# Weights' stream laid out in order of use and loaded two units at a time

## What is computed

```
proj = rms_norm(x, norm1_g) @ w_in
x = x + (sigmoid(ga) * (y_diff @ w_diff_o) + sigmoid(gb) * (y_fox @ w_fox_o)) @ w_out
q = rms_norm(x, norm2_g) @ w_query           # 8 heads, two halves of 128
s = einsum(q, sub_keys); top 16 of 128 in each half, top 16 of the 256 sums
act = gelu(t . expert_u[e]);  x = x + sum_e gate_e * act_e * expert_v[e]     # 8 * 16 = 128 experts a token
...
```

```
x_l = half_ffn(x_l); x_c = half_ffn(x_c)      # 1024 -> 2816 -> 1024, silu gate, adaptive shift and scale
h = rmsnorm(x) * (1 + scale) + shift
y = fourier_na_mixer(h_l, h_c)  in layer 0, mla_mixer(h_l, h_c) in layer 1
x = x + gate * y;  half_ffn again
...
return rmsnorm(x_l, final_g)
```

## Time and profile before

| | |
|---|---|
| median of 3 runs | 3260.35 us (3255.09 to 3262.51) |
| the profiled execution's own time | 3251.68 us |
| its span in the trace | 3249.5 us |
| PE, PEld, DVE, ACT, POOL busy | 91%, 74%, 73%, 31%, 40% |
| moved by DMA | 1003.54 MB, mean 309 GB/s |
| layer 0, gather stage | about 248 to 1066 us |
| layer 1, gather stage | about 1309 to 2176 us |
| second block, latent stream | about 2176 us to the end |

### The profile page before, as it was taken

One profiled execution on the slowest core, in us unless ns is written; L12 is line 12 of the kernel. 1 busy time (PEld: TensorE's weight loads), 2 busy tenths in 40 slices (PEclk: granted clock), 3 DMA queues, 4 the chain that ended last, 5 costly groups with the idle time before them and its releaser, 6 DMA issues. The chain is left out here.

```text
span 3249.5 us, 43549 instructions
## 1 busy us (share of the span) xinstructions
PE 2965.4 (91%) x15748; PEld 2389.1 (74%) x15748; DVE 2362.0 (73%) x4772; ACT 1013.7 (31%) x2036; POOL 1311.5 (40%) x1213
## 2 busy tenths in 40 slices
PE   8998989887887899989997998959999999999998
PEld 5876656564544587767765776729997999997898
DVE  5776777777886776777778877777754787856574
ACT  2422311111241242221111111135455544445543
POOL 1106776677777211667776777660000010000000
PEclk9999999999998999999998999969999999999999
DMA  9659999999999867999999999987761787851453
GB/s 355 224 199 383 360 409 409 409 409 406 385 391 389 327 235 272 373 385 409 409 409 408 395 409 409 408 330 233 232 227 45 243 284 231 274 170 66 158 185 99
DMA packets 276500, 1003.54 MB, mean 309 GB/s; under 512 B 31952, under 2 KB 32752, under 8 KB 276032
## 3 DMA queue, kind: packets, MB, share of 16 engines
q0 software_dynamic: 173696, 635.85, 50.7%
q1 hardware_dynamic: 100944, 361.15, 31.2%
q10 hardware_dynamic: 1648, 3.78, 0.3%
HBM read 999.57 MB, written 1.05 MB: 308 GB/s over the span
## 5 line engine op out<-in xcount | busy, mean ns | idle before, releaser
L289 PE MATMUL bank<-hT,ring 128*128 128x256 f32 x3744 | 835.4, 381 | 13.4 <-ACT hT L929 9.5
L289 PEld LDWEIGHTS bank<-hT,ring 128*128 128x128 f32 x3744 | 714.2, 191 | 142.8 <-issue 37.9
L415 POOL DMA_INDIRECT gring<-in_expert_u,idx x512 | 658.3, 1286 | 376.0 <-PE bank L585 145.0
L1387 DVE CUSTOM_DVE_ANT_0 gring<-gring,t_tok 128x1024 f32<-128x1024 f32 x512 | 611.8, 1225 | 91.0 <-DMA gring<-in_expert_u,idx 69.0
L585 PE MATMUL bank<-gring,dg 128*128 128x512 f32 x1012 | 517.4, 657 | 135.9 <-DMA gring<-in_expert_v,idx 108.7
L415 POOL DMA_INDIRECT gring<-in_expert_v,idx x512 | 554.8, 1084 | 175.2 <-issue 151.4
L1706 DVE TENSOR_TENSOR wl<-ring,wr 128x1024 fp32r<-128x1024 f32 x309 | 377.4, 1223 | 209.5 <-ACT wr L1701 209.2
L585 PEld LDWEIGHTS bank<-gring,dg 128*128 128x128 f32 x1012 | 205.1, 210 | 383.8 <-issue 354.9
L1367 DVE SCALAR_TENSOR_TENSOR x<-gring,wts,x 128x1024 f32<-128x1024 f32 x259 | 332.5, 1284 | 210.7 <-DMA gring<-in_expert_v,idx 142.4
L1710 PE MATMUL bank<-hr,wr 128*128 128x258 f32 (+1 forms) x1512 | 430.1, 284 | 0.8 <-DVE hT L1691 0.6
L1712 PE MATMUL bank<-hr,wl 128*128 128x258 f32 (+1 forms) x1512 | 426.7, 282 | 0.0
(11 more groups left out here) (330 smaller groups left out, 3673.1 us busy)
## 6 DMA issues: line engine op xcount, KB each, us to landing
ring<-in_stream SPq DMA_DIRECT2D x679, 512.0 KB
lat_ada<-in_ada POOLq DMA_DIRECT2D x66, 512.0 KB, 5.4
t_tok<-in_ada POOLq DMA_DIRECT2D x56, 512.0 KB, 5.4
gring<-in_ada POOLq DMA_DIRECT2D x56, 512.0 KB, 6.1
gring<-in_expert_u,idx POOLq DMA_INDIRECT x512
gring<-in_expert_v,idx POOLq DMA_INDIRECT x512
na_bias_sb<-in_na_bias POOLq DMA_DIRECT2D x1, 4096.0 KB, 15.5
x<-in_x SPq DMA_DIRECT2D x2, 512.0 KB, 4.3
```

The lines of the kernel that those rows point to most:

```text
L289: last = pe.matmul(out, w[:, k * P:(k + 1) * P], act_T[:, k, :], start=(k == 0), stop=(k == KD - 1))
L415: pool.indirect_dma_start(out=gring[:, N % GR, :], out_offset=None, in_=table, in_offset=bass.IndirectOffsetOnAxis(ap=idx[:, b, 4 * (Q % 3 ...
L1387: dve.tensor_tensor_reduce(out=rows, in0=rows, in1=t_tok[:, b, :], scale=1.0, scalar=0.0, op0=ALU.mult, op1=ALU.add, accum_out=pre[:, Q % ...
```

## The change

The host now writes `stream` in the order of use: one row for every use, so a unit that is used twice stands there twice, and the rows are put together in pairs, as `[pair, partition, 2, 1024]`. One transfer loads a pair, 8 KB per partition, contiguous in HBM and in SBUF. The ring has eight places, which are four pairs, and one semaphore per pair (`units_full`). SP loads the first four pairs, then the constants, and for every further pair v it waits until both units of pair v-4 are used up. 679 units make 340 transfers, the last with one unit twice. No other engine's instructions change but for the semaphore that is waited for.

```diff
-RING = 9
+RING = 8
+RP = RING // 2
...
-        slot_full = [sem(f"slot_full{i}") for i in range(RING)]
+        units_full = [sem(f"units_full{i}") for i in range(RP)]
...
             u = first[name] + t
-            eng.wait_ge(slot_full[u % RING], 16 * (u // RING + 1))
+            eng.wait_ge(units_full[u // 2 % RP], 16 * (u // RING + 1))
             return ring[:, u % RING, :]
...
-            for u, (row, split, value) in enumerate(order):
-                if u == RING:
+            for v in range((len(order) + 1) // 2):
+                if v == RP:
...
-                if u >= RING:
-                    _, old_split, old_value = order[u - RING]
-                    sp.wait_ge(w_low if old_split else unit_done, old_value)
-                sp.dma_start(ring[:, u % RING, :], io["stream"][row]).then_inc(slot_full[u % RING], 16)
+                if v >= RP:
+                    (split0, value0), (split1, value1) = order[2 * (v - RP):2 * (v - RP) + 2]
+                    if split0 != split1:
+                        sp.wait_ge(w_low if split0 else unit_done, value0)
+                    sp.wait_ge(w_low if split1 else unit_done, value1)
+                at = 2 * (v % RP)
+                sp.dma_start(ring[:, at:at + 2, :], io["stream"][v]).then_inc(units_full[v % RP], 16)
...
-            act.wait_ge(slot_full[u % RING], 16 * (u // RING + 1))
+            act.wait_ge(units_full[u // 2 % RP], 16 * (u // RING + 1))
...
-    io = {"stream": np.concatenate(list(parts.values()), 0)}
+    rows = [place[src] + t for _, src, n, _ in PLAN for t in range(n)]
+    rows += rows[-1:] * (len(rows) % 2)
+    stream = np.concatenate(list(parts.values()), 0)[np.array(rows)]
+    io = {"stream": stream.reshape(-1, 2, P, UW).transpose(0, 2, 1, 3)}
```

More of the change, by code:

```diff
@@ L141, in scored_at, with program @@
     return 2 * b + h if h < EARLY_HEADS else 2 * h + b
-def program(nc, io, place):
+def program(nc, io):
     with ExitStack() as ctx:
@@ L159, in program @@
                 n_raw, n_split = n_raw + (not split), n_split + split
-                order.append((place[src] + t, split, n_split if split else n_raw))
+                order.append((split, n_split if split else n_raw))
         x_in = [sem(f"x_in{b}") for b in range(NB)]
@@ L1613, in program @@
         S0 = tuple(split_before[f"up{F}"] for F in range(4))
-        split_units = [u for u, (_, split, _) in enumerate(order) if split]
+        split_units = [u for u, (split, _) in enumerate(order) if split]
         def late_loads(pool):
@@ L2461, in _layout @@
     io["final_g"] = _cols(v["final_g_2"])
-    return {k_: np.ascontiguousarray(a_) for k_, a_ in io.items()}, place
+    return {k_: np.ascontiguousarray(a_) for k_, a_ in io.items()}
 def kernel(**inputs):
@@ L2467 @@
     from concourse.bass_utils import run_bass_kernel_spmd
-    arrays, place = _layout({k: np.asarray(v) for k, v in inputs.items()})
+    arrays = _layout({k: np.asarray(v) for k, v in inputs.items()})
     nc = bacc.Bacc("TRN2", target_bir_lowering=False, num_devices=1)
@@ L2472 @@
     io["out"] = nc.dram_tensor("out_0", (P, KD, S), F32, kind="ExternalOutput").ap()
-    program(nc, io, place)
+    program(nc, io)
     r = run_bass_kernel_spmd(nc, [{"in_" + n: a for n, a in arrays.items()}], core_ids=[0])
```

## The result

The changed kernel takes **3277.2 us** (median of 5 runs, 3273.9 to 3280.0); the kernel before, run beside it, 3259.0 us (5 runs, 3255.1 to 3262.5). The ratio is 1.0053, 95% interval 1.0039 to 1.0067: 18 us, or 0.53%, slower. The forecast was 3266.5 with a range to 3280; the direction and the range hold, but the loss is three times the forecast one, and the number is nearly that of rival (3). So the question is whether the starved gathers of that rival are the cause, or something else. One execution of a later kernel (single8) took 3971.0 us at a mean granted clock of 0.71 where all others had about 0.96; the ratios leave it out.

What follows compares the result with a forecast made beforehand. DMA was taken to bound the gather stages, PE 8 to 11% behind. Profiled 3251.7 + 13.8 (waits, clock) - 7.5 (larger packets) = 3258.0 us; with 8.7 from profiled to median, 3266.5 was forecast, range 3252 to 3280.

Steps and rivals of the forecast that it cites:

- rival (3): Gather stages: bursts of pairs starve the gathers, raising PE's waits for rows; a tenth gives +12 us, 3278 us; chance 15%.
- The wait at `wq`: Ahead of `wq` 0 and 1, PE stands still for the pair's load: 4.9 us in each layer, 9.8 us together.
- The clock: Behind the new wait at `wq`, PE runs at 0.50 for a while: +2.0 us a layer, +4 us, ends 0 and 5.
- Passes on whole to the first gather: From `wq` through scores and choice to POOL's first gather, no slack: all +13.8 us delays the gather stages, ends 9 and 16.
- Rival (2): PE's later idle times, 8.00 and 5.02 us, absorb the delay, up to 5 to 7 us a layer; chance 25%.
- The DMA's time per byte: Gather stages: 8 KB packets cut the stream's DMA time by 4%, 10.6 us, of which -7.5 us is won; ends 0, -13.
- That they grow: Gather stages: growth of PE's waits for gathered rows was named as a sign that the forecast is wrong.
- Rival (4): Stream transfers: they are cut into 4 KB packets after all, so no gain, 3274 us; chance 5%.
- rival (5): Gather stages: PE takes the DMA's gain back, 3274 us; chance 8%.
- Rival (6): All stream loads: fixed parts paid in line, so halving the loads saves 0.9 us a unit, -180 us, 3080; chance 2%.
- `vv` to `dq` costs nothing: Layer 1 projections: 10.1 us between `vv` 0 and 1 used up and `dq` 0 wanted covers the 7.4 us load.
- The start: First eight units: same order as before, first of a pair seen one unit later, 1.3 us once at most, counted as nothing.

Runs made afterwards that it cites:

- single8: Kernel before with stream stored in order of use and a ring of eight units, each loaded alone: 3255.4 us, +3.9 over the kernel before, ratio 1.0010.
- the repeat: The changed kernel run and profiled once more, no edit, on another chip: 3266.5 us, +15.3 us over the kernel before.
- pair_4k: Changed kernel with a pair's two units one behind the other in HBM, so 1 MB transfers have 4 KB packets: 3268.1 us, +16.7 over the kernel before.
- start_single: Changed kernel with only layer 0's `vv`, the stream's first eight units, loaded one by one: 3266.1 us, +14.9 over the kernel before.
- wq_single: Changed kernel with only the units of `wq` loaded one by one: 3258.0 us, +6.8 over the kernel before, ratio 1.0021.
- layout9: Kernel before with only its stream stored in order of use, nine units loaded alone in 4 KB packets: 3251.0 us, ratio 0.9999.
- triple9: hybrid9 with three units per transfer (12 KB per partition) in the gather stages instead of pairs: 3248.4 us, -2.8 against the kernel before, ratio 0.9990.
- hybrid9: Ring of nine, order-of-use layout, pairs only for units streamed in the gather stages, singles elsewhere: 3245.1 us, 5.7 under the kernel before, ratio 0.9984.
- ou_dq_single: Changed kernel with `ou` 0 and 1 used up first on both blocks, and layer 1's `dq` to `gt` loaded singly: 3251.4 us, +0.6 over the kernel before.
- pairs_dq: single8 with only layer 1's `dq` to `gt` loaded in pairs: 3262.9 us, +12.1 over the kernel before, ratio 1.0036.

## Why the prediction was right or wrong

**The wait at `wq`: right, twice.** 4.9 us were worked out from the hump of one load and the full rate for the second half; 4.89 and 4.92 were measured, 4.87 and 4.85 in the repeat. In the repeat the pair is asked for at 235.20 and PE starts at 240.04. Once PE waits for a load, only the load's own time counts, and that could be read from slices.

**The clock: right in kind and about right in size.** +2.0 us a layer was the forecast, 1.59 (5.32 - 3.73) in the repeat, 1.56 and 2.06 in the first profile. Over all eight such waits (those of pair_4k and start_single too) it is 1.50 to 3.01, mean 1.9. The granted clock was 0.54 in the window of 3.5 us behind the wait, so most of it at 1.2 GHz (0.50 in each us from 240 to 243, 0.90 in the next). After the 0.87 and 0.53 us waits of single8 it stayed at 1.00.

**"Passes on whole to the first gather": right.** wq_single gives back 4.2 us at PE, 4.3 at the gather and 8.5 in the median. Rival (2), that a later idle time takes the delay up, falls, and with it its ground: the 8.00 and 5.02 us of the earlier trace rows were stops of that execution, and the wait that stands near them in the other profiles is one for gathered rows, which come later when the first gather does (the products on them begin at 271.75 in layout9 and at 279.22 in the repeat).

**The DMA's time per byte: right.** From 450 to 750 the stream's queue (packets, MB, share) in layout9, in the changed kernel's repeat, and in triple9:

```profile
q1 hardware_dynamic: 6894, 25.10, 21.0%
```

```profile
q1 hardware_dynamic: 3312, 24.12, 19.4%
```

```profile
q1 hardware_dynamic: 2304, 25.17, 20.0%
```

That is 0.837, 0.804 and 0.795% for each MB: 3.9% less with 8 KB packets, for the 4% that I took, and 5.0% with 12 KB. pair_4k has 20.2% for 24.12 MB, 0.837: it is the packet's size, not the transfer's. By the stage lengths of the table, which scatter, the mean over the seven profiles with 8 KB packets in both stages is 812.6 and 861.0 us, and over the four with 4 KB (layout9, single8, pair_4k, pairs_dq) 814.4 and 864.9: 5.6 us in sum, with some 4 us either way, for the 7.5 forecast. Before and the first profile of the changed kernel are left out for their stops. hybrid9, which has this gain and nothing else, says 5.7 us by medians. So the time per byte was right, and what was kept of it a little less than forecast. The first profile does not show the gain: its two stages are 14 us longer than the repeat's; how much of this its stops make is not shown.

**Starved gathers, rival (3): not the cause,** though its number came close. Its place was the gather stages, and these are shorter with 8 KB packets, not longer. PE's waits for gathered rows in 1350 to 2100 are 34.3 us in the first profile of the changed kernel and 36.6 in the repeat, 29.6 in before, and 36.7 in layout9, which has 4 KB packets and nine singles. That they grow was named as a sign that the forecast is wrong; against before alone they do, but so they do with nothing changed but the order in HBM. Rival (4) falls by the packets, 52128 on q1 in the whole span where layout9 has 100944, and rival (5) by hybrid9's gain. Rival (6) is far from every number.

**"`vv` to `dq` costs nothing": this step failed.** I had asked whether PE would have `dq` in time, with 10.1 us of cover for 7.4, and it had: in the repeat its 128 products there take 27.79 us as in before. The question I did not ask was who else loads then. POOL fetches `ada` in pieces of 512 KB that DVE consumes as they land, and DVE has no slack: the forget gates stand behind these products on DVE, and PE waits for them already in before, 3.68 us. When both units of a pair come free, 1 MB of the stream is put beside these loads at once. DVE's waits for `ada` go from 2.8 us (layout9) to 7.9 (repeat), PE's for the gates from 3.29 to 8.10, **+4.8 us**. ou_dq_single and pairs_dq show it from both sides. In layer 0 DVE's waits grow too (1.6 to 2.5 us), but PE's wait for the gates stays 0.42 us: there DVE has slack.

The Trainium skill has a sentence near the 2.0 us by which 8 KB packets are worse than 4 KB ones here ("DMA: Bandwidth & Descriptors", section "Queues, rings and completion order"): an engine goes round its queues packet by packet. But a packet there is typically a group of 9 to 17 descriptors, and what this document calls a packet is a single run of bytes. So the sentence by itself gives no reason for 6.10 us in pair_4k and 8.10 in the repeat, and no run here shows the turns themselves; why the size of the run matters to a neighbour stays open. The same page wants at least 1 MiB per DMA (section "Rules for kernel authors"). By the trace this gives nothing in these stages: pair_4k moves 1 MB at a time and shows 409 GB/s, as the 512 KB pieces do. The fixed 2 us that the prediction took from that page of the Trainium skill, its section on the anatomy of a DMA, is given there for transfers issued from GpSimd, and the stream is issued from SP; nothing in the sum rested on it.

**The sum with what was measured,** changed kernel's repeat against layout9, by the rows and the table: start 1.9 (PE would begin `wq` at 235.17 without its wait, 240.04 - 4.87, for 233.23 in layout9), wait and clock 6.5 in layer 0 (8.4 at the first gather in all), stage of layer 0 -4.8, forget gates +4.8, wait and clock 6.4 in layer 1, 0.7 unexplained between the stages, stage of layer 1 -0.9: 14.6 with rounding, for 14.7 between the spans. Forecast had been 13.8 - 7.5 = 6.3. The waits came out 0.9 lower, the gain 1.8 smaller in this pair of profiles, and 4.8 + 1.9 + 0.7 were not in it. The start is the least sure. I had allowed it 1.3 at most and put it at nothing. Of its 1.9 us 1.5 are the late start of PE behind `norm1_g` (12.32 for 10.79), and pair_4k, without that, is ready for `wq` at 233.06 (238.05 - 4.99); yet start_single, without it too, is so only at 234.37, and its median won only 0.4. The gain was forecast from 10.6 us, of which three quarters are 7.9 and not 7.5; and 24.84 us over 80 packets are 0.311 each, not 0.312. Neither slip changes a reading.

**The range held in part by luck.** The ends of the prediction's own terms, 16 us of waits and no gain, reach to some 3276.4 us (3260.4 + 16); 3277.2 lies beyond that, and inside the range only because its upper end was set for rival (3), which was not the cause. The repeat's +15.3 us stay within those ends, but by waits that were not among the terms.

What stays open: why the first group showed +18 us and the repeat +15.3 by medians. Both are within the interval of 13 to 22 us that the ratio gives, and the stops seen in the first group may have a part in it.

## What to carry to other kernels

When loads are joined, look not only at the consumer of the joined load, but at every other transfer that is short of time at that moment: here twice the bytes at once, and larger packets, delayed whoever loaded beside them, `ada` in layer 1 and `norm1_g` at the start. Join them only in the stages in which the DMA's bytes set the time, and keep single units where each is waited for; here that turned 0.5% slower into 0.16% faster. A ring shortened by one unit shows its price mostly at the one place where a unit is asked for just before its use, and what matters there is the time from release to landing of the whole joined piece.

## What the runs showed of the hardware

Packets of 4 KB move at 409 GB/s in stages that DMA fills, with 8 KB for the stream, a fifth to a quarter of the bytes, at 412; with 12 KB the window from 400 to 780 stayed at 412 and the time did not fall. Waits of PE of 0.5 to 1.2 us in layer 0 left its clock at 1.00 (single8, wq_single); behind waits of 4.9 us it stood at 0.50 for 3 to 4 us in the two profiles of the changed kernel and for 6 us once in pair_4k. A load of 512 KB took 6.8 us (median) from issue to landing in layout9's gather stage, and 3.3 to 4.5 where the DMA engines had little else (230 to 245). Beside 1 MB loads with 8 KB packets an 8 KB load of another queue landed in 7.6 to 8.1 us, beside the same loads with 4 KB packets in 6.6. And a stop of 5 to 9 us stood in two profiled executions and in none of twelve others: an idle time with a releaser that makes no sense should be looked for in a second profile before a rival is built on it.
